# Seven products of halves in place of eight: the retention's input projection in a two-block kernel

## What is computed

```
def retention_module(h, positions, w_in, w_out):
    proj = h @ w_in
    q, k, v, g = jnp.split(proj, [qk_w, 2 * qk_w, 2 * qk_w + D_INNER], axis=-1)
...
    q = apply_rotary(q, cos, sin)
    k = apply_rotary(k, cos, sin) * (RET_QK_DIM ** -0.5)
...
    scores = jnp.einsum("bnihd,bnjhd->bnhij", qc, kc) * inner_decay
...
    return (jax.nn.silu(g) * o) @ w_out
```

## Time and profile before

| | us |
|---|---|
| median of three timed runs | 3027.72 |
| lowest and highest of them | 3022.31, 3029.49 |
| the profiled execution, its time | 3021.74 |
| the profiled execution, its span | 3019.9 |
| PE busy in it | 2708.0 |
| the retention's input projection on PE, L1108 | 329.9 |

### The profile page before, as it was taken

How to read it: one execution, slowest core, us unless ns; L and a number is a source line. 1 busy time by engine, 2 the same in 40 slices (tenths; PEclk the granted TensorE clock), 3 DMA queues, 4 the chain that set the end, 5 groups by cost and what they waited for, 6 DMA issues and landing times.

```text
span 3019.9 us, 32561 instructions
## 1 busy us (share of the span) xinstructions
PE 2708.0 (90%) x11116; PEld 1206.9 (40%) x11116; DVE 1102.2 (36%) x2207; ACT 460.0 (15%) x884; POOL 316.7 (10%) x445
## 2 busy tenths in 40 slices
PE   7999999999998999989789899886989699999963
PEld 3444444444444446544433233232544333333321
DVE  4999970320003023376731111114556521111104
ACT  3111131100101010352101000002153000101000
POOL 0101112000000000000122111110000121121110
PEclk9999999999999999989899999997999799999986
DMA  6656341222210211002489999996201699999993
GB/s 224 221 180 198 125 182 58 79 78 84 84 60 24 95 56 56 28 1 72 162 305 394 394 393 392 393 381 231 79 23 51 224 374 392 379 351 332 361 339 134
DMA packets 272217, 603.10 MB, mean 200 GB/s; under 512 B 18437, under 2 KB 43333, under 8 KB 272001
## 3 DMA queue, kind: packets, MB, share of 16 engines
q1 hardware_dynamic: 256864, 580.70, 52.6%
q0 software_dynamic: 15264, 21.24, 2.0%
HBM read 743.04 MB, written 29.20 MB: 256 GB/s over the span
## 4 chain that ended last, share of the span: by engine, by line
PE 70%; SPq 11%; DMA 7%; DVE 6%; issue 2%; ACT 2%; POOL 0%; POOLq 0%; DVEq 0%; ACTq 0%
PE psum L1021 11%; PE psum L1411 11%; PE psum L1108 11%; SPq L654 9%; PE psum L1243 9%; PE psum L1079 7%; DMA arena<-in_w 6%; PE psum L1433 4%; PE psum L1348 4%; PE psum L1279 2%; PE psum L1006 1%; PE psum L1129 1%; PE psum L1290 1%; PE psum L1301 1%; PE psum L1398 1%
## 5 line engine op out<-in xcount | busy, mean ns | idle before, releaser
L1411 PE MATMUL psum<-arena 128*64 128x512 f32 x2656 | 637.8, 625 | 88.3 <-DMA arena<-in_w 86.5
L1411 PEld LDWEIGHTS psum<-arena 128*64 128x64 f32 x2656 | 191.0, 143 | 415.2 <-issue 410.0
L1021 PE MATMUL psum<-arena 128*128 128x512 f32 x768 | 342.2, 601 | 2.6 <-ACTq L751 2.6
L1108 PE MATMUL psum<-arena 128*128 128x512 f32 x768 | 329.9, 592 | 0.8 <-ACT arena L730 0.8
L1433 PE MATMUL psum<-arena 128*64 128x512 f32 x1328 | 302.6, 599 | 0.1
L1510 DVE SCALAR_TENSOR_TENSOR arena<-arena 128x512 f32<-128x512 f32 x451 | 300.1, 745 | 0.0
L1243 PE MATMUL psum<-arena 128*128 128x512 f32 (+1 forms) x800 | 288.5, 520 | 5.4 <-ACT arena L817 5.4
L1079 PE MATMUL psum<-arena 128*128 128x512 f32 x512 | 224.4, 601 | 5.2 <-POOL arena L2231 4.4
L1108 PEld LDWEIGHTS psum<-arena 128*128 128x128 f32 x768 | 145.9, 190 | 184.2 <-issue 183.2
L1021 PEld LDWEIGHTS psum<-arena 128*128 128x128 f32 x768 | 143.9, 191 | 177.7 <-issue 174.8
L1243 PEld LDWEIGHTS psum<-arena 128*128 128x128 f32 x800 | 151.4, 191 | 129.0 <-issue 113.6
(11 more groups left out here) (294 smaller groups left out, 2043.6 us busy)
## 6 DMA issues: line engine op xcount, KB each, us to landing
arena<-in_w SPq DMA_DIRECT2D x261, 2048.0 KB, 18.5
arena<-in_w_ada SPq DMA_DIRECT2D x48, 1024.0 KB, 5.2
arena<-in_conv_w_in SPq DMA_DIRECT2D x24, 1024.0 KB
arena<-in_ret_w_in SPq DMA_DIRECT2D x12, 2048.0 KB, 8.1
arena<-in_w_in SPq DMA_DIRECT2D x8, 2048.0 KB, 9.1
arena<-moe_out SPq DMA_DIRECT2D x10, 1024.0 KB, 10.0
arena<-in_conv_w_out SPq DMA_DIRECT2D x4, 2048.0 KB, 12.0
arena<-in_ret_w_out SPq DMA_DIRECT2D x4, 2048.0 KB, 7.8
```

The lines of the kernel that those rows point to most:

```text
L1021: m = pe.matmul(bank(b + c), w[:, k, c * P:(c + 1) * P], c_hT[:, k, :], start=(k == 0), stop=(k == KD - 1))
L1108: m = pe.matmul(bank(4 * (n % 2) + j), l_, r_, start=(k == 0), stop=(k == KD - 1))
L1411: m = pe.matmul(bank(2 * s)[part], m_xsT[s][:, at:at + SB], m_w[s][j][:, k, :], start=(k == 0), stop=(k == KD - 1))
```

## The change

For the first eleven of the twelve chunks the product is done by Strassen's scheme. Weights and input are cut in halves in both directions: of the eight k the first four and the last four, of the 512 columns (or tokens) the first and the last 256. A chunk is then a 2 x 2 by 2 x 2 product of such blocks, and instead of eight products of blocks seven are computed, of blocks or of sums of blocks, in the variant with 15 sums. A product is 2 x 4 matmuls of 128 x 128 by 128 x 256, and fills one bank.

The sums are spread so: four of the weights for each chunk on GpSimd (two into buffers `r_sa`, two in place in the ring's slot), four of the input once for all chunks on VectorE (`r_ta`), and seven of the results for each chunk, which VectorE does as it reads the products' banks. ScalarE copies product 1 out. The queries and keys are turned after that, from SBUF, each quarter of the chunk when it is done. The gate's SiLU is taken in place in SBUF, quarter by quarter. Chunk 11 stays as it was. Banks are now taken in a circle of eight, seven for each chunk.

Two things move: the transfer of the decay table goes from before the stage to behind the second load of the out-projection's weights, since its place holds sums of the input; and VectorE's small gain vectors (`gains`) are worked out after chunk 4 instead of chunk 3.

The core of the diff:

```diff
+        HT, NW = S // 2, 11
+        R_PRODUCTS = (1, 2, 5, 6, 7, 4, 3)
...
             for n in range(S_ROUT, S_ROUT + 4):
                 load(n)
+                if n == S_ROUT + 1:
+                    sp.wait_ge(sem("ri_mm"), ri_mm(NW - 1, 3))
+                    sp.dma_start(mem(W0 + 16384, RH * S), a["decay"]).then_inc(sem("pos_in"), 16)
...
+            for n in range(NW):
+                act.wait_ge(sem("ri_mm"), ri_mm(n, 1))
+                if 1 <= n < 4:
+                    act.wait_ge(sem("ri_dve"), ri_dve(n - 1, "u4"))
+                act.activation(r_quarter(n, 0, 0), bank(7 * n % 8).rearrange("p (m n) -> p m n", m=2), ACT.Copy)\
+                    .then_inc(sem("ri_act"), 1)
+                if n >= 8:
+                    for c in R_BLOCKS:
+                        gate = r_quarter(n, int(c[1]) - 1, int(c[2]) - 1)
+                        act.wait_ge(sem("ri_dve"), ri_dve(n, c))
+                        act.activation(gate, gate, ACT.Silu).then_inc(sem("ri_act"), 1)
...
+            def r_product(n, i):
+
+                p, w, x = R_PRODUCTS[i], slot_cols(S_RIN + n), c_hT
+                k0, k1, h0, h1 = slice(0, 4), slice(4, 8), slice(0, HT), slice(HT, S)
+                of_w, of_x = {1: (w[:, k0, h0], x[:, k0, h0]), 2: (w[:, k1, h0], x[:, k1, h0]),
+                              5: (r_sa[n][0], r_ta[0]), 6: (r_sa[n][1], r_ta[1]), 7: (w[:, k0, h1], r_ta[2]),
+                              4: (w[:, k1, h1], r_ta[3]), 3: (w[:, k1, h0], x[:, k1, h1])}[p]
+                if p == 1:
+                    pe.wait_ge(sem(f"st_w{(S_RIN + n) % 3}"), streamed(S_RIN + n))
+                elif p in (5, 6, 7, 3):
+                    pe.wait_ge(sem("ri_sum"), 4 * n + (5, 6, 7, 3).index(p) + 1)
+                if n == 0 and p in (5, 6, 7, 4):
+                    pe.wait_ge(sem("ri_dve"), (5, 6, 7, 4).index(p) + 1)
...
+                to = r_bank_free(n, i)
+                still, moved = (of_x, of_w) if 4 <= n < 8 else (of_w, of_x)
+                for m_ in range(2):
+                    for k in range(4):
+                        m = pe.matmul(to[:, m_ * HT:(m_ + 1) * HT], still[:, k, m_ * P:(m_ + 1) * P], moved[:, k, :],
+                                      start=(k == 0), stop=(k == 3))
+                m.then_inc(sem("ri_mm"), 1)
...
+            def turned_pair(n, i, t):
...
+                link(dve.tensor_tensor(by_cos, pair, both(r_cos), ALU.mult))
+                link(dve.tensor_tensor(by_sin, pair, both(r_sin), ALU.mult))
+                link(dve.tensor_tensor(dst[:, 0, :], by_cos[:, 0, :], by_sin[:, 1, :], ALU.subtract))
+                link(dve.tensor_tensor(dst[:, 1, :], by_sin[:, 0, :], by_cos[:, 1, :], ALU.add))
...
+            def r_sums(n):
+
+                (d11, d12), (d21, d22) = [[r_quarter(n, i, t) for t in range(2)] for i in range(2)]
+                dve.wait_ge(sem("ri_act"), ri_act(n, "p1"))
+                r_sum(n, "u2", 6, d22, d11)
+                r_sum(n, "c11", 2, d11, d11)
+                if n < 4:
+                    turned_pair(n, 0, 0)
+                r_sum(n, "u4", 5, d12, d22)
+                r_sum(n, "u3", 7, d21, d22)
+                r_sum(n, "c22", 5, d22, d21)
+                if n < 4:
+                    turned_pair(n, 1, 1)
+                r_sum(n, "c21", 4, d21, d21)
...
+                r_sum(n, "c12", 3, d12, d12)
...
+            for n in range(NW):
+                w, (s1, s2) = slot_cols(S_RIN + n), r_sa[n]
+                w11, w12 = w[:, 0:4, 0:HT], w[:, 4:8, 0:HT]
+                w21, w22 = w[:, 0:4, HT:S], w[:, 4:8, HT:S]
+                pool.wait_ge(sem(f"st_w{(S_RIN + n) % 3}"), streamed(S_RIN + n))
+                if n >= 2:
+                    pool.wait_ge(sem("ri_mm"), ri_mm(n - 2, 6))
+                pool.tensor_tensor(s1, w21, w22, ALU.add).then_inc(sem("ri_sum"), 1)
+                pool.wait_ge(sem("ri_sum"), 4 * n + 1)
+                pool.tensor_tensor(s2, s1, w11, ALU.subtract).then_inc(sem("ri_sum"), 1)
+                pool.tensor_tensor(w21, w11, w21, ALU.subtract).then_inc(sem("ri_sum"), 1)
+                pool.wait_ge(sem("ri_sum"), 4 * n + 2)
+                pool.wait_ge(sem("ri_mm"), ri_mm(n, 2))
+                pool.tensor_tensor(w12, w12, s2, ALU.subtract).then_inc(sem("ri_sum"), 1)
```

More of the change, by code:

```diff
@@ L789, in _ @@
             act.activation(r_sin, r_sin, ACT.Sin).then_inc(sem("rot"), 1)
[L790 to L799, removed]
+            for n in range(NW):
[9 more added lines that the diff above has]
+                        act.activation(gate, gate, ACT.Silu).then_inc(sem("ri_act"), 1)
+            for j in range(4):
+                act.wait_ge(sem("ri_mm"), ri_mm(NW, j))
+                act.activation(mem(r_g + S * (4 * (NW - 8) + j), S), bank((7 * NW + j) % 8), ACT.Silu)\
+                    .then_inc(sem("ri_act"), 1)
             for h in range(RH):
@@ L1093, in _, with r_bank_free @@
             pe.wait_ge(sem("rms_hT"), past("rms_hT", 1) + KD)
[L1094 to L1097, removed]
-                    pe.wait_ge(sem("cols"), 1)
[L1099 to L1109, removed]
+            def r_bank_free(n, i):
+                q = 7 * n + i - 8
+                if q >= 0:
+                    n_, p_ = q // 7, R_PRODUCTS[q % 7]
+                    if p_ == 1:
+                        pe.wait_ge(sem("ri_act"), ri_act(n_, "p1"))
+                    else:
+                        pe.wait_ge(sem("ri_dve"), ri_dve(n_, R_READ_LAST[p_]))
+                return bank((7 * n + i) % 8)
@@ new lines, in _ @@
+            for n in range(NW):
+                for i in range(7):
+                    r_product(n, i)
+            pe.wait_ge(sem(f"st_w{(S_RIN + NW) % 3}"), streamed(S_RIN + NW))
+            for j in range(4):
+                to = r_bank_free(NW, j)
+                for k in range(KD):
+                    m = pe.matmul(to, slot_cols(S_RIN + NW)[:, k, j * P:(j + 1) * P], c_hT[:, k, :],
+                                  start=(k == 0), stop=(k == KD - 1))
+                m.then_inc(sem("ri_mm"), 1)
@@ L1565, in _ @@
             normalise(1, r_xn)
[L1567 removed]
+            dve.wait_ge(sem("pos_in"), 32)
             C1, C2 = 6.28125, 1.9340515136718750e-3
@@ new lines, in gains @@
+            def gains():
+                dve.wait_ge(sem("cols"), 1)
+                dve.wait_ge(sem("cols_in"), 64)
+                for q, l, sc, sh, n in ((0, 0, 1, 0, 8), (1, 0, 4, 3, 0), (2, 1, 1, 0, 2), (3, 1, 4, 3, 4)):
+                    for who in range(2 if q < 3 else 1):
+                        g, b = hx_cols(q, who)
+                        scale, shift = mod_col(who, l, sc), mod_col(who, l, sh)
+                        if q == 0:
+                            link(dve.tensor_copy(b, shift))
+                        else:
+                            link(dve.scalar_tensor_tensor(out=b, in0=scale, scalar=1.0, in1=ln_col(n + 1),
+                                                          op0=ALU.add, op1=ALU.mult))
+                            link(dve.tensor_tensor(b, b, shift, ALU.add))
+                        if q == 0 and who == 1:
+                            link(dve.tensor_scalar(g, scale, 1.0, None, ALU.add))
+                        else:
+                            link(dve.scalar_tensor_tensor(out=g, in0=scale, scalar=1.0, in1=ln_col(n),
+                                                          op0=ALU.add, op1=ALU.mult))
+                dve.sem_inc(sem("row_norm"), 1)
@@ L1620, in _ @@
+            for n in range(NW):
+                r_sums(n)
+                if n == 4:
+                    gains()
             dve.wait_ge(sem("pos_in"), 48)
```

88 lines of the change are left out of this document (49 added, 39 removed).

## The result

| | before | changed |
|---|---|---|
| median, us | 3025.01 (4 runs) | 2990.23 (4 runs) |
| lowest and highest | 3021.5, 3029.49 | 2985.16, 2990.98 |
| the profiled execution | 3021.74 | 2989.95 |
| ratio of the runs, 95% interval | 1 | 0.9881 (0.9869 to 0.9892) |

A forecast was written before the change was run, and what follows sets the result against it. The prediction took PE, busy for 90% of the span, to bound the kernel. The mean of four runs, 3025.3 us, less 36.1 for the narrower records gives 2989.2, plus 1 for waits: forecast 2990 us, range 2983 to 2999.

The forecast's parts named there:

- The bound: Retention's in-projection: one unbroken 329.88 us of PE at clock 1.00, scores following within 0.7 us, so PE time saved shortens the whole.
- The record's price: PE in the in-projection: a 256-column matmul record costs 216 ns, so eleven chunks give -36.1 us.
- the dear end: PE in the in-projection: other end of the price, 221 ns a record, 6.2 us less gain over 1232 records.
- The cover of a weight load: PE's weight loads: a load of 190 ns inside a record of 216 ns leaves 26 ns of cover.
- The rival that rested on it: In-projection: weight loads become the pace; no gain at 245 ns a record, 3044 at 260; slower by either bound, chance 0.03.
- Its extreme of 3092 us: In-projection: no overlap of loads at all, 528 more loads x 190 ns against 36 us of columns, 64 us longer.
- GpSimd's sums: GpSimd in the in-projection: four sums a chunk at 2.53 us, 10.1 us against PE's 24.2, hidden, cost nothing.
- the rival with a factor of three: GpSimd becomes the bound: sums at 7.5 us each, 30 us a chunk, 3053; slower by either bound, chance 0.03.
- The cover is gone when a sum takes over 6 us: GpSimd's four sums a chunk stay hidden behind PE up to 4 x 6.05 = 24.2 us.
- 14.9 + 10.1 = 25.0 us: Vector engine's chunk if all rotary operations and GpSimd sums excluded each other: 0.8 us over PE's, in four chunks, absorbed by banks.
- stays at 0.69 us: Vector engine beside GpSimd: its operation keeps 0.69 us, while a GpSimd operation starting beside it takes 0.4 us longer.
- The 1 us that I added for 77 waits: PE in the in-projection: 1 us added to the forecast for what 77 waits ahead of products may show.

The follow-up runs named there:

- halves: The kernel before, each bank of the retention's in-projection filled by two passes of 256-column matmuls in place of one of 512, no sums: 3023.6 us, ratio 0.9997.
- six: The changed kernel with the scheme for chunks 0 to 5 only, chunks 6 to 11 done as before: 3006.15 us, ratio 0.9941 against the kernel before.
- quarters: The kernel before, each bank of the retention's in-projection filled by four passes of 128-column matmuls: 3044.3 us, ratio 1.0066.
- sums12_late: The changed kernel with eight more GpSimd sums a chunk, for chunks 5 to 10 only: 3015.5 us, ratio 0.997 against the kernel before.
- sums8: The changed kernel with GpSimd's first sum of each chunk done five times, 8 sums a chunk: 3008.7 us, ratio 0.9948 against the kernel before.
- sums12: The changed kernel with GpSimd's first sum of each chunk done nine times, 12 sums a chunk: 3058.4 us, ratio 1.011 against the kernel before.

## Why the prediction was right, and where it was not

- **The bound.** PE without a gap, a clock of 1.00, and the scores right behind: right. The stage's 36.2 us came off the end of the chain; in the profiled pair 31.8 are left, because the profile of the kernel before had the second block's rarer, shorter kind.
- **The record's price.** 216 ns from four tiles was the term on which everything rested, and 216.1 ns was measured over 1232 records; 221 ns, the dear end, was not touched. `halves` shows the same price without any sums, `six` shows that it scales with the chunks.
- **The cover of a weight load.** "A weight load of 190 ns inside a record of 216 ns leaves 26 ns of cover" is wrong. `quarters` ran at 111.8 ns a record with loads of the same 190 ns. The rival that rested on it, slower from 245 ns a record, had less to stand on than its part of the 0.03. Its extreme of 3092 us was also priced too low: it counts 190 ns for the 528 added loads, while the prediction's own 403 ns for all 1232 records gives some 230 us more, near 3220; and the band in which the difference stays within 9 us is 238 to 252 ns, not 237 to 253. The Trainium skill, "TensorE: Matmul & The Clock Gate", section "The mechanism" (the prediction named the section behind it), says of small tiles that share the array that a load overlaps matmuls only where its row group differs. Taken as a rule for these full-array loads it does not hold: by it 3092 us, measured 2990.
- **GpSimd's sums.** 2.35 us each where 2.53 were taken (L2250's mean), also where an operand is four rows of 256 apart from each other, so the rival with a factor of three fell. The fourth sum of a chunk ends 11 us ahead of its product (582.5 against 593.5 in chunk 0), the three others 19 to 21 us ahead. The placement in the queue was right. "The cover is gone when a sum takes over 6 us" is right where nothing is rotated (`sums12_late`, 28.8 us a chunk) and wrong beside the rotation of chunks 0 to 3: there eight sums of 2.4 us, 19 us of 24, already cost PE 9.2 us of waiting.
- **The vector engine.** The step that failed, without a price in this kernel, is the bound "14.9 + 10.1 = 25.0 us": I added the lengths of both engines' work as if each exclusion cost its own length. What happens is a turn for each instruction, so a short operation pays a whole GpSimd sum. I had also read that VectorE's operation "stays at 0.69 us" beside GpSimd; there it had started first and GpSimd was the one to wait. In the changed kernel VectorE comes second and pays 0.92 us, in each of the four chunks. It stayed at that because GpSimd's three sums for the next chunk end at 589.53, before the second rotary operation; with four more sums behind them, in `sums8`, it did not.
- **The sum.** 36.1 us against 36.2 in the stage; 2990 against a median of 2990.2. The 1 us that I added for 77 waits was not there: they cost nothing. The mean of four runs was a better base than the profiled run, 3.5 us lower, whose second block had its shorter kind. That the total agrees to 0.2 us is luck: single runs of either kernel scatter by 3 to 4 us, and the needless 1 us made up for a gain of the medians 1.4 us below the stage's.

## What to carry to other kernels

Count a matmul stage by its moving columns: at 256 columns a record twice as many matmuls cost 2 us of 330, at 128 columns four times as many cost 13, and a scheme that trades columns for sums on idle engines gives nearly the whole eighth (24.2 us a chunk for 27.5). When you hide work on GpSimd beside the vector engine, count the vector operations with two SBUF inputs, not their time: each can be made to wait for a whole GpSimd instruction, and some with one SBUF input can too. Repeating a hidden step two and three times shows how far its cover reaches before one relies on it.

## What the runs showed of the hardware that was not expected

- GpSimd and VectorE take turns, beside GpSimd's sums in SBUF, also for very short operations: a 256-element operation with two SBUF inputs of 0.43 us took 2.46 us, and eight-element operations of 0.17 us beside the sums of `sums8` took 2.2 to 2.3 us, every second one of a row of them. Two with one SBUF input are among them: L1711, 2.27 us, and in `sums12` a copy (L1705), 1.75 us.
- A weight load's PEld duration of 190 ns is not its price: 3072 of them in 343 us.
- Behind a short wait of PE the clock stayed up, behind a longer one it fell. In `sums12_late` PE ran 112 records in 24.44 us behind waits of 2.03 and 1.82 us, and in 26.74 and 26.98 us behind waits of 4.42 and 4.33 us; unbroken they take 24.2. In `sums12` a wait of 2.99 us was still followed by 24.41 us, and one of 8.07 us cost 1.7 us behind it, no more than one of 4.07 (1.9 us). The first 5 us behind them, PEclk third from the end:

```profile
731.66:736.66 5.00, 5.00 (x13) 4.05 (x14) 0.00 (x0) 0.00 (x0) 4.97 (x3) 0.53 0.00 0
...
760.43:765.43 5.00, 5.00 (x23) 4.43 (x24) 0.00 (x0) 0.00 (x0) 4.97 (x3) 1.00 0.01 3
789.21:794.21 5.00, 5.00 (x12) 4.01 (x13) 0.00 (x0) 0.00 (x0) 4.98 (x3) 0.50 0.01 3
```

  0.53 and 0.50 are the lower of the clock's two levels, 1.2 GHz, behind the long waits; behind the wait of 2.03 us it stays at 2.4 GHz.
